# Decoder layer with 32 experts: the scatter products of an expert pair placed between the weight blocks of the next pair's gate/up product

## The chip, the cores and the metric

The kernel runs on one core of one Trainium2 chip. The metric is the device time of one execution in microseconds (us); lower is better. The times named as the median are of three executions; the profile is of a fourth one, whose time is given beside its span.

## The reference, cut to what matters

One layer of a decoder is computed for 256 prompt rows and 8 sample rows, T = 264 rows in all, of width 1024. After a convolution, two attentions and two normalisations each row goes to its 4 best of 32 experts. In the kernel the part around the change is the last one:

```python
def moe_ffn(x, w_router, b_router, w_gate_up, b_gate_up, w_down, b_down):
    ...
    logits = (xf @ w_router + b_router).astype(jnp.float32)
    top_logit, top_idx = lax.top_k(logits, TOP_K)
    gates = jax.nn.softmax(top_logit, axis=-1)
    ...
    def expert_block(args):
        xblk, e = args
        gu = xblk @ w_gate_up[e] + b_gate_up[e]
        g, u = jnp.split(gu, 2, axis=-1)
        g = jnp.minimum(g, SWIGLU_LIMIT)
        u = jnp.clip(u, -SWIGLU_LIMIT, SWIGLU_LIMIT)
        act = (u + 1.0) * g * jax.nn.sigmoid(SWIGLU_ALPHA * g)
        return act @ w_down[e] + b_down[e]
    ...
    y = jnp.zeros((T + 1, D_MODEL), yb.dtype).at[buf_tok].add(yb * buf_gate[:, None].astype(yb.dtype))
```

All is in float32. The gate/up weights of one expert are 1024 x 2048 numbers, 8 MB, and the down weights 1024 x 1024, 4 MB.

## The kernel before

Ahead of the experts the kernel computes the dense layers and the attentions; the change doesn't touch them. Then it works through the experts in 16 pairs. An expert has 64 slots for rows, so a pair fills the 128 partitions of one tile. For each pair, TensorE (PE) does this, in the function `pair(r, j)`, with `it = 2 * r + j`:

- gate/up of the first expert (`gate_up`, L1730): first a small bf16 product for the bias, then 8 blocks c = 0 to 7. A block is one loaded item of 1 MB of weights, and 4 matmuls with 512 columns each, two beside each other in the two halves of the array's columns. They add up in PSUM banks 0 and 1.
- the scatter (`scatter`, L1762): 8 products, c = 0 to 7. Each takes 128 of the 1024 output columns of the pair before (`yb`, copied from PSUM by ScalarE, ACT) and spreads them with the selection matrix `SelT` to the 264 rows of the layer. They use PSUM banks 2 and 3 in turn. VectorE (DVE) adds each one to the running sum `xT` (`add_scattered`, L1350), and product c waits until the addition of product c - 2 is done (semaphore `e_y_out`).
- 3 small transposes that make the next `SelT` (L1797), 4 transposes of the activations of the first expert (`turn_act`, L1739), which ACT copies to `actT` (L917), and then `down` (L1752): 4 items of 1 MB, 8 matmuls' worth of each half.
- gate/up of the second expert, then the gathering of the rows of the next pair (`gather`, L1702 and L1704), `turn_act`, and `down` of the second expert.

DVE works in the order in which its loop is written: for the first expert `clamp` (L1333 writes g2, L1335 writes u2) and `swiglu` (L1339, L1343), then `add_scattered`, then the copies of `SelT` (L1363 to L1365), the next selection matrices, then `clamp` and `swiglu` of the second expert. ACT computes the sigmoid between them (L911). `clamp` waits for `e_gu`, which the last matmul of gate/up raises; `turn_act` waits for `e_act`, which L1343 raises. So the order on DVE decides when PE gets the additions and when it gets the activations.

The weights come by DMA from the sync queue (SP). There are 16 items of room. `round_loads` walks over the items in order: before item m it waits in `item_read` until PE is through with the item that lay there (`e_wu` after each of the blocks 0 to 6, `e_gu` after block 7, `e_du` and `e_dn` for down). An expert has 12 items, all experts together 384, and the first 16 are loaded before the experts start. SP's order is fixed: while it waits for one item's room it issues nothing behind it.

In the last pair (`last=True`) the gathering is left out, and `sum_turned` (L1776) lays the running sum into the PSUM banks of the last normalisation.

Of the kernel before, what the change touches and what calls it, by code (L numbers as in the profile page):

```python
# [25 lines left out]
P = 128  # L26
D = 1024
DC = D // P
NP_ = 256
NS = 8  # L30
T = NP_ + NS
# [105 lines left out]
def decoder_layer(nc, x_prompt, x_sample, mem_prompt, cache_win_k, cache_win_v, state_conv, cache_mem_k,  # L137
# [4 lines left out]
    with ctx:  # L142
# [15 lines left out]
        ps = ctx.enter_context(nc.psum_tensor("ps", [P, 8, 512], F32))  # L158
# [115 lines left out]
        yb = view(m0 + 3584, 2, 512)  # L274
# [655 lines left out]
        def _(dve):  # L930
# [424 lines left out]
                dve.sem_inc(first, 1)  # L1355
            pairs = dve.value_load(nswi[0:1, 0:1], min_val=16, max_val=80)
            with dve.Fori(0, pairs) as it:
                clamp(2 * it)
                swiglu(2 * it)
                add_scattered(it)  # L1360

                dve.wait_ge(e_st, it + 1)
                nc.vector.tensor_copy(SelT[:, 0, :], ps[:, 3, 0:T]).then_inc(e_st_out, 1)  # L1363
                nc.vector.tensor_copy(SelT[0:64, 1, :], ps[64:P, 3, 0:T]).then_inc(e_st_out, 1)
                nc.vector.tensor_copy(SelT[64:P, 1, :], ps[0:64, 3, 0:T]).then_inc(e_st_out, 1)  # L1365

                q = ((it + 1) % 16) * 2
                dve.wait_ge(e_pos, it + 1)
                dve.wait_ge(e_selg, it + 1)
                select(q)  # L1370
                advance(q, it + 2)
                clamp(2 * it + 1)
                pick_biases(q)
                swiglu(2 * it + 1)
# [5 lines left out]
        def _(pe):  # L1380
# [334 lines left out]
            ins.then_inc(s_rt, 1)  # L1715
            pe.wait_ge(s_nsw, 4)

            def gate_up(r, k):


                a = k % 2
                for c in range(-1, 8):
                    if c >= 0:
                        item_arrived(pe, r, PER_EXPERT * k + c)
                        w, x = expert_slot(PER_EXPERT * k + c), xTe[:, c, SLOTS * a:SLOTS * a + SLOTS]
                    else:
                        w, x = bgu3[0:3 * NX, :], selE[0:3 * NX, a, :]
                    for gu in range(2):
                        for j in range(2):
                            ins = mm(ps[64 * j:64 * j + 64, gu, :], x,  # L1730
                                     w[:, D * gu + 512 * j:D * gu + 512 * j + 512], start=(c < 0), stop=(c == 7),
                                     skip_group_check=True)
                    if 0 <= c < 7:
                        ins.then_inc(e_wu, 1)
                ins.then_inc(e_gu, 1)

            def turn_act():
                for q in range(4):
# [14 lines left out]
                                     start=(m == 0), stop=(m == 7), skip_group_check=True)  # L1753
                    ins.then_inc(e_du if i < 3 else e_dn, 1)

            def scatter():

                for c in range(DC):
                    half = c // 4
                    if c >= 2:  # L1760
                        pe.wait_ge(e_y_out, scattered[0] + c)
                    mm(ps[:, 2 + c % 2, 0:T], yb[:, half, P * (c % 4):P * (c % 4) + P], SelT[:, half, :],  # L1762
                       start=True, stop=True).then_inc(e_y, 1)

            scattered = [0]
            pe.sem_inc(e_at, 1)
            pairs = pe.value_load(nswi[0:1, 0:1], min_val=16, max_val=80)
            last_round = pe.value_load(nswi[0:1, 2:3], min_val=7, max_val=39)
# [10 lines left out]
            def pair(r, j, last=False):  # L1779

                it = 2 * r + j
                scattered[0] = DC * it
                pe.wait_ge(e_gx_out, it + 1)
                pe.wait_ge(e_sb, it + 1)
                pe.wait_ge(e_u2, 2 * it + 1)
                gate_up(r, 2 * j)
                pe.wait_ge(s_first, 16)
                pe.wait_ge(s_rt_out, 6)
                pe.wait_ge(s_alpha, 1)
                pe.wait_ge(e_yb, it + 1)  # L1790
                pe.wait_ge(e_st_out, 3 * it + 1)
                pe.wait_ge(e_at_out, 2 * it + 1)
                scatter()
                pe.wait_ge(e_y_out, DC * it + (DC + 1))
                pe.wait_ge(e_selg, it + 1)
                for t, (t0, n) in enumerate(TCH):
                    ins = tp(ps[:, 3, t0:t0 + n], SelG[0:n, t].rearrange("p a s -> p (a s)"), ident[0:n, 0:n])  # L1797
                ins.then_inc(e_st, 1)
                pe.wait_ge(e_act, 2 * it + 2)
                turn_act()  # L1800
                pe.wait_ge(e_at_out, 2 * it + 2)
                down(r, 2 * j)
                if last:
                    sum_turned(0, 0)
                    sum_turned(0, 1)
                    pe.wait_ge(e_st_out, 3 * it + 4)
                    sum_turned(1, 1)
                pe.wait_ge(e_u2, 2 * it + 2)
                gate_up(r, 2 * j + 1)
                if last:  # L1810
                    pe.wait_ge(e_u2, 2 * it + 3)
                    sum_turned(2, 0)
                    sum_turned(2, 1)
                else:
                    pe.wait_ge(e_sel, it + 2)
                    gather()
                pe.wait_ge(e_act, 2 * it + 3)
                turn_act()
                pe.wait_ge(e_at_out, 2 * it + 3)
                if last:  # L1820
                    sum_turned(1, 0)
                down(r, 2 * j + 1)
# [44 lines left out]
```

## Time and profile before

| | us |
|---|---|
| median of 3 runs | 1408.44 |
| the three runs | 1408.44, 1399.79, 1411.55 |
| the profiled execution | 1414.02 |
| its span | 1412.1 |
| PE busy | 1224.5 (87% of the span) |
| DVE busy | 376.2 (27%) |
| ACT busy | 210.1 (15%) |
| mean granted clock of TensorE | 0.954 of full speed |
| moved from HBM | 479.40 MB |

The profiled execution took 1.9 us more than its span, and 5.6 us more than the median. Busy shares are means over stages that have different limits, so they say little by themselves: which wait ends last in a stage has to be read from the chain of waits and from the timeline of that stage. Line numbers are those of the kernel before. A float32 matmul leaves two records in the trace, so that a block of 4 matmuls is 8 records and a scatter product 2; their durations overlap, and some records are missing.

### The profile page before, as it was taken

How to read it: one execution, taken by the hardware profiler on the slowest of the kernel's cores; microseconds unless marked ns; L12 is line 12 of the kernel's file. 1: busy time of each engine (PE TensorE's matmuls, PEld its weight loads, DVE VectorE, ACT ScalarE, POOL GpSimd, SP SyncE). 2: the span in 40 equal slices, each digit the busy share in tenths (PEclk: the TensorE clock that was granted, in tenths of full speed). 3: DMA queues.
4: the chain of work that ended last, by engine and by line, in shares of the span. 5: the costliest groups of instructions: out<-in, count | busy, mean ns of one | idle time of the engine just before them, and what ended most of it. 6: DMA issues, size and time to landing. Idle time of an engine off the chain costs nothing.

```text
span 1412.1 us, 16873 instructions
## 1 busy us (share of the span) xinstructions
PE 1224.5 (87%) x6509; PEld 617.4 (44%) x6509; DVE 376.2 (27%) x843; ACT 210.1 (15%) x370; POOL 78.8 (6%) x61
## 2 busy tenths in 40 slices
PE   3896997995887999999899998999889898898986
PEld 2894443874674334333433343333433333333332
DVE  3365433117325221202212032021220202212023
ACT  3441222022312010010110101101001010100001
POOL 2014300004001000000000000000000000000001
PEclk7998999998997999999999999999999999999999
DMA  9885799515991999999999999999999999999993
GB/s 289 178 255 164 181 164 337 179 65 201 364 417 74 364 418 416 416 419 417 419 418 416 417 419 417 419 417 416 418 419 418 419 417 416 418 418 418 417 416 130
DMA packets 104709, 487.17 MB, mean 345 GB/s; under 512 B 8948, under 2 KB 10636, under 8 KB 71296
## 3 DMA queue, kind: packets, MB, share of 16 engines
q1 hardware_dynamic: 99296, 469.47, 85.3%
q0 software_dynamic: 3824, 15.62, 4.2%
q10 hardware_dynamic: 1552, 1.57, 0.4%
q8 instruction: 25, 0.41, 0.1%
q14 instruction: 12, 0.10, 0.0%
HBM read 479.40 MB, written 7.24 MB: 345 GB/s over the span
## 4 chain that ended last, share of the span: by engine, by line
PE 56%; SPq 24%; DVE 9%; issue 4%; ACT 3%; DMA 3%; POOL 1%; DVEq 0%; POOLq 0%
PE ps L1730 19%; SPq L569 13%; SPq L565 11%; PE ps L1433 11%; PE ps L1752 10%; PE ps L1464 4%; PE ps L1762 3%; PE ps L1702 2%; DMA ring<-in_w_gate_up_dram 2%; PE ps L1583 1%; DVE arena L1350 1%; DVE ring L1064 1%; ACT arena L917 1%; PE ps L1418 1%; DMA arena<-in_b_gate_up_dram 1%
## 5 line engine op out<-in xcount | busy, mean ns | idle before, releaser
L1730 PE MATMUL ps<-ring,arena 128*64 128x512 f32 x1536 | 340.1, 594 | 11.7 <-DMA ring<-in_w_gate_up_dram 11.7
L1333 DVE TENSOR_SCALAR arena<-ps 128x512 f32<-128x512 f32 x32 | 22.2, 693 | 703.0 <-PE ps L1730 703.0
L1730 PEld LDWEIGHTS ps<-ring,arena 128*64 128x64 f32 x1536 | 108.8, 137 | 228.1 <-issue 188.4
L1752 PE MATMUL ps<-ring,arena 128*64 128x512 f32 x768 | 170.1, 596 | 22.6 <-ACT arena L917 22.6
L1762 PE MATMUL ps<-arena 128*128 128x264 f32 x256 | 92.4, 507 | 34.5 <-DVE arena L1350 33.6
L1752 PEld LDWEIGHTS ps<-ring,arena 128*64 128x64 f32 x768 | 53.1, 137 | 124.2 <-issue 95.9
L911 ACT ACTIVATE arena<-arena 128x512 f32<-128x512 f32 x32 | 20.2, 632 | 578.3 <-DVE arena L1333 578.3
L1433 PE MATMUL ps<-arena,ring 128*128 128x264 f32 x384 | 89.2, 395 | 5.1 <-DVE arena L1120 3.7
L1464 PE MATMUL ps<-x_split,w_split 128*128 128x264 f32 x576 | 75.0, 294 | 21.1 <-DVE w_split L949 21.1
L1762 PEld LDWEIGHTS ps<-arena 128*128 128x128 f32 x256 | 52.2, 239 | 80.5 <-DVE arena L1350 62.6
L1730 PE MATMUL ps<-late,arena 128*64 128x512 f32 x384 | 85.3, 593 | 0.3 <-DMA late<-in_w_gate_up_dram 0.3
L1464 PEld LDWEIGHTS ps<-x_split,w_split 128*128 128x128 f32 x576 | 73.7, 197 | 22.1 <-issue 14.7
L1433 PEld LDWEIGHTS ps<-arena,ring 128*128 128x128 f32 x384 | 74.5, 195 | 19.2 <-DVE arena L1120 3.9
L1350 DVE TENSOR_TENSOR arena<-arena,ps 128x264 f32<-128x264 f32 x128 | 53.6, 429 | 36.3 <-PE ps L1762 35.2
L1702 PE MATMUL ps<-arena 128*128 128x128 bf16 x768 | 55.5, 225 | 8.2 <-DVE arena L1313 8.2
L1433 PE MATMUL ps<-ring,arena 128*128 128x512 f32 x128 | 60.4, 628 | 0.0
L1702 PEld LDWEIGHTS ps<-arena 128*128 128x128 bf16 x768 | 50.8, 101 | 20.4 <-issue 20.4
L730 POOL TENSOR_TENSOR late<-late,arena 128x1024 f32<-128x1024 f32 x1 | 2.0, 1994 | 960.5 <-ACT late L848 960.5
L1730 PEld LDWEIGHTS ps<-late,arena 128*64 128x64 f32 x384 | 27.5, 137 | 55.4 <-issue 53.6
L1730 PE MATMUL ps<-arena 96*64 96x512 bf16 (+1 forms) x256 | 48.2, 486 | 0.9 <-ACT arena L906 0.9
L669 POOL TENSOR_TENSOR ring<-ring 128x1536 f32<-128x1536 f32 (+1 forms) x11 | 42.3, 3858 | 47.3 <-DMA ring<-in_cache_win_k_dram 25.1
L949 DVE TENSOR_TENSOR w_split<-ring,w_split 128x1024 fp32r<-128x1024 f32 x24 | 35.4, 1484 | 35.2 <-ACT w_split L758 35.1
(264 smaller groups left out, 990.6 us busy)
## 6 DMA issues: line engine op xcount, KB each, us to landing
ring<-in_w_gate_up_dram SPq DMA_DIRECT2D x192, 1024.0 KB, 20.5
ring<-in_w_down_dram SPq DMA_DIRECT2D x96, 1024.0 KB, 24.4
late<-in_w_gate_up_dram SPq DMA_DIRECT2D x48, 1024.0 KB, 19.3
late<-in_w_down_dram SPq DMA_DIRECT2D x24, 1024.0 KB, 23.4
arena<-in_w_gate_up_dram SPq DMA_DIRECT2D x16, 1024.0 KB, 19.2
ring<-in_w_in_dram SPq DMA_DIRECT2D x12, 1024.0 KB, 22.2
ring<-in_cache_mem_k_dram SPq DMA_DIRECT2D x8, 1024.0 KB, 4.9
ring<-in_cache_mem_v_dram SPq DMA_DIRECT2D x8, 1024.0 KB, 8.1
```

The costliest lines, as they stand in the source:

```text
L565: sp.dma_start(dst, src).then_inc(done, 16)
L569: sp.dma_start(dst.rearrange("p (k n) -> p k n", k=2), src).then_inc(done, 16)
L669: nc.gpsimd.tensor_tensor(k, k, q.unsqueeze(1).broadcast_to((P, 2, width)), ALU.mult).then_inc(s_kq, 1)
L949: nc.vector.tensor_tensor(w_lo[p % 2], win_piece(p), w_hi[p % 2].bitcast(F32), ALU.subtract).then_inc(s_wlo, 1)
L1333: nc.vector.tensor_scalar(g2, ps[:, 0, :], 7.0, None, ALU.min).then_inc(e_g2, 1)
L1350: nc.vector.tensor_tensor(xT[:, c, :], xT[:, c, :], ps[:, 2 + c % 2, 0:T], ALU.add).then_inc(e_y_out, 1)
L1433: ins = mm(out(n), lhs(w, k, kk), rhs(w, k, kk), start=(kk == 0), stop=(kk == 7))
L1464: ins = mm(ps[:, n % 4, 0:T], w[p % 2][:, cols], x[kk], start=(kk == 0 and m == 0), stop=(kk == 7 and m == 2))
L1702: mm(out, x3[:, t, k, P * c:P * c + P], Sel[:, t].rearrange("p a s -> p (a s)"), start=(t == 0 and k == 0), stop=False)
L1730: ins = mm(ps[64 * j:64 * j + 64, gu, :], x, w[:, D * gu + 512 * j:D * gu + 512 * j + 512], start=(c < 0), stop=(c == 7), skip_group_check ...
L1752: ins = mm(ps[64 * j:64 * j + 64, 4 + half, :], x, w[:, kk, 512 * half:512 * half + 512], start=(m == 0), stop=(m == 7), skip_group_check= ...
L1762: mm(ps[:, 2 + c % 2, 0:T], yb[:, half, P * (c % 4):P * (c % 4) + P], SelT[:, half, :], start=True, stop=True).then_inc(e_y, 1)
```

## The change

The 8 scatter products leave their place behind the gate/up product of the first expert and go between its blocks: product c - 1 stands behind block c, for c = 1 to 7, and the product 7 behind product 6 at the end. `e_gu` is still raised by the last matmul of block 7, ahead of the products 6 and 7. The waits that stood ahead of the scatter (for `yb`, `SelT` and the first values) now stand ahead of product 0, behind block 1. On DVE `add_scattered(it)` moves ahead of `clamp(2 * it)`. The numbers of the instructions and what they compute stay the same; so do the orders of SP and ACT.

```diff
--- before.py
+++ after.py
@@ -1355,9 +1355,9 @@
                 dve.sem_inc(first, 1)
             pairs = dve.value_load(nswi[0:1, 0:1], min_val=16, max_val=80)
             with dve.Fori(0, pairs) as it:
+                add_scattered(it)
                 clamp(2 * it)
                 swiglu(2 * it)
-                add_scattered(it)
 
                 dve.wait_ge(e_st, it + 1)
                 nc.vector.tensor_copy(SelT[:, 0, :], ps[:, 3, 0:T]).then_inc(e_st_out, 1)
@@ -1715,7 +1715,7 @@
             ins.then_inc(s_rt, 1)
             pe.wait_ge(s_nsw, 4)
 
-            def gate_up(r, k):
+            def gate_up(r, k, scattered=None):
 
 
                 a = k % 2
@@ -1732,7 +1732,12 @@
                                      skip_group_check=True)
                     if 0 <= c < 7:
                         ins.then_inc(e_wu, 1)
-                ins.then_inc(e_gu, 1)
+                    if c == 7:
+                        ins.then_inc(e_gu, 1)
+                    if scattered is not None and c > 0:
+                        scatter(scattered, c - 1)
+                if scattered is not None:
+                    scatter(scattered, DC - 1)
 
             def turn_act():
                 for q in range(4):
@@ -1753,16 +1758,21 @@
                                      start=(m == 0), stop=(m == 7), skip_group_check=True)
                     ins.then_inc(e_du if i < 3 else e_dn, 1)
 
-            def scatter():
-
-                for c in range(DC):
-                    half = c // 4
-                    if c >= 2:
-                        pe.wait_ge(e_y_out, scattered[0] + c)
-                    mm(ps[:, 2 + c % 2, 0:T], yb[:, half, P * (c % 4):P * (c % 4) + P], SelT[:, half, :],
-                       start=True, stop=True).then_inc(e_y, 1)
-
-            scattered = [0]
+            def scatter(it, c):
+
+                half = c // 4
+                if c == 0:
+                    pe.wait_ge(s_first, 16)
+                    pe.wait_ge(s_rt_out, 6)
+                    pe.wait_ge(s_alpha, 1)
+                    pe.wait_ge(e_yb, it + 1)
+                    pe.wait_ge(e_st_out, 3 * it + 1)
+                    pe.wait_ge(e_at_out, 2 * it + 1)
+                if c >= 2:
+                    pe.wait_ge(e_y_out, DC * it + c)
+                mm(ps[:, 2 + c % 2, 0:T], yb[:, half, P * (c % 4):P * (c % 4) + P], SelT[:, half, :],
+                   start=True, stop=True).then_inc(e_y, 1)
+
             pe.sem_inc(e_at, 1)
             pairs = pe.value_load(nswi[0:1, 0:1], min_val=16, max_val=80)
             last_round = pe.value_load(nswi[0:1, 2:3], min_val=7, max_val=39)
@@ -1779,18 +1789,10 @@
             def pair(r, j, last=False):
 
                 it = 2 * r + j
-                scattered[0] = DC * it
                 pe.wait_ge(e_gx_out, it + 1)
                 pe.wait_ge(e_sb, it + 1)
                 pe.wait_ge(e_u2, 2 * it + 1)
-                gate_up(r, 2 * j)
-                pe.wait_ge(s_first, 16)
-                pe.wait_ge(s_rt_out, 6)
-                pe.wait_ge(s_alpha, 1)
-                pe.wait_ge(e_yb, it + 1)
-                pe.wait_ge(e_st_out, 3 * it + 1)
-                pe.wait_ge(e_at_out, 2 * it + 1)
-                scatter()
+                gate_up(r, 2 * j, scattered=it)
                 pe.wait_ge(e_y_out, DC * it + (DC + 1))
                 pe.wait_ge(e_selg, it + 1)
                 for t, (t0, n) in enumerate(TCH):
```

PE, the first pair as it stands ahead of the loop's repetition, before: the blocks of gate/up (L1730), then the scatter (L1762; L1761 and L497 are the reckoning of the values waited for).

```order
238 L1730 MATMUL ps<-ring,arena 64x512 x8
239 L497 REGISTER_ALU
240 L1730 MATMUL ps<-ring,arena 64x512 x4
241 L1791 ISA
242 L1762 MATMUL ps<-arena 128x264 x2
243 L1761 ISA
244 L1762 MATMUL ps<-arena 128x264
245 L1761 REGISTER_ALU
246 L1762 MATMUL ps<-arena 128x264
247 L1761 REGISTER_ALU
248 L1762 MATMUL ps<-arena 128x264
```

All 8 products stand together behind the last block. PE, the same place of the changed kernel, where the scatter's line is L1773 and its waits are L1769 and L1772:

```order
234 L1730 MATMUL ps<-late,arena 64x512 x4
235 L1769 ISA
236 L1773 MATMUL ps<-arena 128x264
237 L1730 MATMUL ps<-late,arena 64x512 x4
238 L1773 MATMUL ps<-arena 128x264
239 L1730 MATMUL ps<-late,arena 64x512 x4
240 L1772 ISA
241 L1773 MATMUL ps<-arena 128x264
...
254 L1730 MATMUL ps<-ring,arena 64x512 x4
255 L1772 REGISTER_ALU
256 L1773 MATMUL ps<-arena 128x264
258 L1773 MATMUL ps<-arena 128x264
```

Six of the products have moved ahead of the last block, and two follow it. DVE, the start of its loop over the pairs, before: the clamps and the activation (L1333 to L1343), then the additions (L1350).

```order
344 L1333 TENSOR_SCALAR arena<-ps 128x512
345 L1335 TENSOR_SCALAR arena<-ps 128x512
346 L1338 REGISTER_ALU
347 L1339 SCALAR_TENSOR_TENSOR arena<-arena 128x512
348 L1343 TENSOR_TENSOR arena<-arena 128x512
349 L1347 ISA
350 L1350 TENSOR_TENSOR arena<-arena,ps 128x264
351 L1349 REGISTER_ALU
352 L1350 TENSOR_TENSOR arena<-arena,ps 128x264
```

DVE, the end of the additions and what follows them in the changed kernel:

```order
356 L1350 TENSOR_TENSOR arena<-arena,ps 128x264
357 L1349 REGISTER_ALU
358 L1350 TENSOR_TENSOR arena<-arena,ps 128x264
359 L1332 ISA
360 L1333 TENSOR_SCALAR arena<-ps 128x512
361 L1335 TENSOR_SCALAR arena<-ps 128x512
362 L1338 REGISTER_ALU
363 L1339 SCALAR_TENSOR_TENSOR arena<-arena 128x512
364 L1343 TENSOR_TENSOR arena<-arena 128x512
365 L1362 REGISTER_ALU
```

The eight additions now stand ahead of the clamps of the same pair.

## Rows read from the trace of the kernel before

**Rows 1.** The page, GB/s in 40 equal slices of the span

```profile
GB/s 289 178 255 164 181 164 337 179 65 201 364 417 74 364 418 416 416 419 417 419 418 416 417 419 417 419 417 416 418 419 418 419 417 416 418 418 418 417 416 130
```

**Rows 2.** Busy time by stretch; last columns granted clock, DMA share, GB/s

```profile
600.00:700.00 100.00, 92.23 (x506) 37.52 (x503) 17.19 (x34) 10.71 (x13) 0.00 (x0) 0.98 1.02 418
960.00:1300.00 340.00, 303.20 (x1612) 122.03 (x1612) 66.91 (x138) 33.90 (x42) 0.00 (x0) 0.98 1.02 418
1385.00:1390.00 5.00, 4.32 (x33) 2.91 (x32) 0.99 (x2) 0.59 (x1) 0.00 (x0) 1.00 0.13 50
```

**Rows 3.** The chain of waits: start us, us, what

```profile
849.18 7.09 PE ps L1752 x32
...
877.87 0.73 PE ps L1762 x2
...
907.17 7.09 PE ps L1752 x32
...
1052.88 5.53 SPq L569
...
1113.13 5.54 SPq L569
```

**Rows 4.** Timeline of one pair: start us, us, engine, line, operation, idle before

```profile
869.41 0.14 PEld L1730 LDWEIGHTS ps<-ring,arena 128*64 128x64 f32 x2 [0.28 <-issue]
870.37 1.16 PE L1762 MATMUL ps<-arena 128*128 128x264 f32 x4
870.49 0.69 DVE L1333 TENSOR_SCALAR arena<-ps 128x512 f32<-128x512 f32 x1 [23.38 <-PE ps L1730]
...
872.54 0.69 DVE L1343 TENSOR_TENSOR arena<-arena 128x512 f32<-128x512 f32 x1
...
879.63 0.66 PE L1739 MATMUL ps<-arena 128*128 128x128 f32 x4
...
881.03 1.94 PE L1752 MATMUL ps<-arena 128*64 128x512 f32 x8 [0.75 <-ACT arena L917]
```

**Rows 5.** Timeline of the last pair

```profile
1343.93 1.94 PE L1730 MATMUL ps<-ring,arena 128*64 128x512 f32 x8 [0.55 <-DMA ring<-in_w_gate_up_dram]
...
1346.41 1.94 PE L1730 MATMUL ps<-ring,arena 128*64 128x512 f32 x8 [0.55 <-DMA ring<-in_w_gate_up_dram]
...
1348.28 1.16 PE L1762 MATMUL ps<-arena 128*128 128x264 f32 x4
...
1358.98 1.94 PE L1752 MATMUL ps<-arena 128*64 128x512 f32 x8 [0.75 <-ACT arena L917]
...
1388.89 7.09 PE L1752 MATMUL ps<-ring,arena 128*64 128x512 f32 x32
```

**Rows 6.** Timeline of the first pair, and one stretch of it by busy time

```profile
466.23 1.16 PE L1762 MATMUL ps<-arena 128*128 128x264 f32 x4
...
476.69 7.09 PE L1752 MATMUL ps<-ring,arena 128*64 128x512 f32 x32 [0.68 <-ACT arena L917]
...
478.67 5.48 SPq L565 DMA_DIRECT2D ring<-in_w_gate_up_dram  x4
...
477.00:478.00 1.00, 1.00 (x6) 0.29 (x4) 0.85 (x2) 0.00 (x0) 0.00 (x0) 1.00 0.00 0
```

**Rows 7.** The page's groups: busy us, mean ns of one, idle before

```profile
L1762 PEld LDWEIGHTS ps<-arena 128*128 128x128 f32 x256 | 52.2, 239 | 80.5 <-DVE arena L1350 62.6
...
L1350 DVE TENSOR_TENSOR arena<-arena,ps 128x264 f32<-128x264 f32 x128 | 53.6, 429 | 36.3 <-PE ps L1762 35.2
```

**Rows 8.** Granted clock by stretch, columns as in Rows 2

```profile
873.50:874.00 0.50, 0.37 (x1) 0.32 (x2) 0.41 (x2) 0.00 (x0) 0.00 (x0) 0.86 1.03 426
...
877.00:877.50 0.50, 0.50 (x3) 0.40 (x2) 0.12 (x1) 0.00 (x0) 0.00 (x0) 0.73 1.19 492
```

**Rows 9.** Timeline behind a second expert's down product

```profile
971.95 0.60 PE L1730 MATMUL ps<-arena 96*64 96x512 bf16 x4
972.17 1.01 ACT L922 COPY arena<-ps 128x1024 f32<-128x1024 f32 x1 [7.19 <-PE ps L1752]
```

## The prediction

> **What bounds the kernel now.** I read the page first, then busy time by stretch, then the chain of waits, and last the timelines of a first, a middle and the last expert pair. By its busy share (87%, in the table) PE looks like the bound, but the page's GB/s slices stay at 416 to 419 from the fifteenth slice to the last but one [rows 1]. The stretches say the same: 418 GB/s and a full DMA share both where PE is busy 92.23 of 100 us and where it is busy 303.20 of 340 [rows 2]. The chain shows two regimes. Up to about 960 us it runs through PE, with a pair period of 907.17 - 849.18 = 58.0 us; from there it runs through the sync queue, with a period of 1113.13 - 1052.88 = 60.25 us [rows 3]. A pair has 24 items of 1 MB (1.0486 million bytes): 24 x 1.0486 / 60.25 = 0.418 MB per us, which is the rate of the stretches. So the loads run without a hole, at one item in 2.5 us, from the first pair to about 1386 us, where the DMA share drops to 0.13 [rows 2]. In the first half PE only eats a stock of loaded items faster than it is refilled, and in the second half it waits for weights. Time that PE saves in the middle pairs buys nothing. Only two places count: the **last pair**, where PE works behind the last load it waited for, and the **first pair**, where PE decides when the loads can start again.
>
> **What is around the scatter.** In the pair at 870 us the first two scatter products start at 870.37, at once behind the last block. The third one needs an addition, and DVE makes additions only behind the clamps and the activation. From 870.37 to the start of down at 881.03 it is 10.66 us [rows 4]. In the last pair it is 1358.98 - 1348.28 = 10.70, in the first pair 476.69 - 466.23 = 10.46 [rows 5, 6].
>
> **The new way from the last block to down.** Behind the last block only the products 6 and 7 are left. Two products take 1.16 us to their end [rows 4]. The additions of the products 0 to 5 run beside the blocks, and that of product 7 follows its product with 0.43 us, the mean of an addition [rows 7]. Now DVE may clamp: from the start of L1333 to the end of L1343 it is 872.54 + 0.69 - 870.49 = 2.74 us; then come the turning of the activations and ACT's copy of them, 881.03 - 879.63 = 1.40 us to down [rows 4]. The sum is 1.16 + 0.43 + 2.74 + 1.40 = 5.73, with some hundredths for each hand-over between engines 5.8 us. The three small transposes for `SelT` fit into PE's idle time before the turning. So the additions ahead of the clamp cost the activation 1.5 us, and yet the way is 4.9 us shorter, 4.65 in the first pair.
>
> **The clock takes a part back.** PE is idle between the last scatter or transpose and the turning. Today the same idle, some 2.1 us between the second and third product, is followed by the lower level of the granted clock: from the two half-microsecond rows, 0.86 at 873.5 and 0.73 at 877.0, it stood at 0.50, which is 1.2 GHz, from 873.86 to 877.27, so 3.4 us [rows 8]. The same half-microsecond reading finds this in 13 of the 16 pairs, the first at 471 and the last at 1351.7. In the changed kernel PE is idle from 1.6 + 0.6 = 2.3 us after the last block (transposes done) to 4.4 us, again 2.1 us. I take it that the clock falls there too. 3.4 us at half clock cost at most 1.7 us; the copy by ACT lies in them and costs nothing more. I take 1.4, with 0 and 1.7 as the ends.
>
> **Cost of a product between two blocks.** One product more in a row costs 1.16 - 0.73 = 0.43 us of PE [rows 3, 4]. The change from a block to a product cost 0.10: the weight loads of a block come every 0.43 us, the last at 869.41, and the product starts at 870.37, 0.96 later instead of 0.86 [rows 4]. No row shows a product followed by a block of gate/up; the ends are 0 and another 0.1 to 0.5, and I take 0, since PE's stream goes on without a gap elsewhere. So one insertion is 0.53 us, six are 3.2.
>
> **Last pair.** There PE is paced by the loads: its blocks start at 1343.93 and 1346.41, 2.48 apart, and the next work follows a block's start by 1348.28 - 1346.41 = 1.87 [rows 5]. The free 0.61 us hold a product of 0.43 with 0.18 to spare. So the last block is as late as before, at the same time of the loads, the insertions are free, and the gain is 10.70 - 5.8 - 1.4 = **3.5 us** (3.2 to 4.9). Is something else late next? The 16 items behind that block arrive every 2.48 us, the last at 1346.41 + 39.7 = 1386.1; down of the last expert, which starts at 1388.89 and wants its last item 5.3 us later [rows 5], would start at 1385.4 and want it at 1390.7. For the last expert's gate/up, whose last item arrives at 1346.41 + 12 x 2.48 = 1376.2, there is a margin of a good microsecond. The loads stop the gain only beyond some 5 us.
>
> **First pair.** All 16 items are in when the experts start. The 8 blocks free 8 items; once these are moved the DMA engines stand still (0 GB/s from 477 to 478) until PE has finished the first item of down and SP issues again at 478.67 [rows 6]. Every microsecond by which down starts earlier moves the whole stream of 368 loads. But here PE is not paced by loads, so the insertions count: 4.65 - 3.2 = 1.45 us. With the fallen clock the turning and the first item of down take up to 1.3 us more: **0.15 us** are left (0 to 1.45). The blocks free an item every 1.77 + 0.53 = 2.3 us (down, of the same 1 MB items, takes 7.09 us for four [rows 3]), still under the 2.5 us of a load.
>
> **The 14 pairs between**: nothing. They would save PE 0.2 to 1.5 us each, and PE then waits that much longer for its next item, or eats its stock sooner.
>
> **The waits that moved.** Ahead of product 0 stands the wait for `yb`, with blocks 2 to 7 queued behind it on PE, and SP waits for those blocks. ACT has copied `yb` 1.2 us after gate/up starts (972.17 + 1.01 against 971.95) [rows 9], and product 0 comes two blocks, 4 us, after that start: covered. Without cover each microsecond would cost one in the first pair. `SelT` and `b_down` are older still. DVE stands in the additions while the blocks run; behind them are only the clamps, which need the last block anyway.
>
> **The sum** is 3.5 + 0.15, so about 3.7 us: the profiled execution would go from 1414.02 to 1410.3. That execution is 5.6 above the median of 1408.44; I take the gain off the median: **1404.8 us**.
>
> **The rivals.**
> *The clock stays up* behind the shorter, broken idle, as it did in 3 of 16 pairs. Then the last pair gives 4.9 and the first 1.45, together 6.3 us: 1402.1. Against it: the idle is as long as today.
>
> *The weights' loads show (the slower side).* Each product sits between blocks that use the array in another way. If PE could not load the weights of a product, and those of the next block, behind running matmuls, an insertion would cost two loads of 0.24 [rows 7] and one of 0.14 [rows 4] more, 0.62 us. In the first pair the blocks would end 6 x 0.62 = 3.7 us later and the loads would start again 0.15 - 3.7 = 3.6 us later than today; in the last pair (0.62 - 0.18) x 6 = 2.6 us of the 3.5 would go. The sum is -3.6 + 0.9: 2.7 us slower, 1411.1. It decides from 0.39 us per insertion on, where 3.65 = 6 x 0.39 + 6 x 0.21. Against it speaks the 0.10 us of the change from block to product [rows 4], where the first load was hidden. The Trainium skill, "TensorE: Matmul & The Clock Gate", Part 3, states that a weight load overlaps running matmuls only when it goes to another row group; all operands here use all 128 rows, so by that rule this rival would hold. The rows speak against the rule here.
>
> *PE sets the pace after all.* If the rate of 418 GB/s followed PE's demand, all 16 pairs would count: 16 x 1.45 = 23 us with the clock up, 1385; with the clock down 16 x 0.15 is lost among the rest. Against it: the same rate in both regimes [rows 2]. The Trainium skill, "Perfetto Trace Analysis", section "Optimization Strategies", advises to work on whatever the idle matmul engine waits for; read as a forecast, that advice is this rival, and the equal rates of this trace speak against it.
>
> **How the numbers follow.** Forecast (3 to 4 us) 0.6, clock up 0.2, weight loads shown 0.1, PE's pace 0.03; 0.07 for the rest. The first three span 1402.1 to 1411.1. The runs of one kernel lie between 1399.79 and 1411.55, so a median of a few can be off by some 4 us to either side; the slow case and a late run together are rare, and I give 1397 to 1412. About 1% (14 us) is what a measurement of this kernel can tell from no change: all cases but the pace of PE are within it. Faster by over 1%: 0.05; within 1%: 0.92; slower by over 1%: 0.03.
>
> **What would show it.** In the profile after: in the last pair down starts 5.8 to 7.5 us behind the last block; six products lie in the waits for loads, and the blocks there stay 2.48 us apart; the GB/s slices stay at 418, the chain goes over to the sync queue earlier than 960 us, and the second half's period stays at 60.25. In the first pair the hole without loads ends at about the same time. The clock falls once per pair, now at the turning. The forecast is wrong if the loads run faster than 418 GB/s, if blocks are further apart than 2.48 in the last pair, or if the end of the loads moves by more than 2 us.

## The result, and the profile after

The changed kernel takes 1435.03 us (median of 4 runs, 1430.61 to 1438.22) against 1406.33 for the kernel before (4 runs, 1399.79 to 1411.55). The ratio is 1.0208, with a 95% interval of 1.0166 to 1.025: it is slower by 2%, where no measurable change was forecast (1404.8 us, with a range of 1397 to 1412). The profiled execution took 1430.61 us, its span is 1428.7. All times and ratios here and below are of executions in the fast state; one of the ten of experiment 4 (2865.66 us, mean granted clock 0.449) was in the slow state and is not in its ratio.

The page of the changed kernel: busy time, GB/s in 40 slices, the costliest groups of gate/up and down, and the median time from issue to landing of a gate/up item.

```profile
PE 1254.8 (88%) x6509; PEld 600.9 (42%) x6509; DVE 374.4 (26%) x843; ACT 210.0 (15%) x370; POOL 78.6 (6%) x61
...
GB/s 289 177 256 153 183 194 360 119 89 221 408 350 162 361 416 411 418 418 418 416 417 418 418 418 416 417 418 419 418 417 417 418 419 418 418 416 417 417 273 31
...
L1730 PE MATMUL ps<-ring,arena 128*64 128x512 f32 x1536 | 351.3, 597 | 0.0
L1757 PE MATMUL ps<-ring,arena 128*64 128x512 f32 x768 | 187.1, 644 | 22.6 <-ACT arena L917 22.6
...
ring<-in_w_gate_up_dram SPq DMA_DIRECT2D x192, 1024.0 KB, 11.6
```

The rate of the loads is the same as in [rows 1], and yet the last two slices fall to 273 and 31: the last weights land at 1382.8 us, 46 us before the kernel ends. In the kernel before they landed at 1386.9, 25 us before its end. Gate/up (L1730) has no idle time before its matmuls now; in the kernel before this group waited 11.7 us for loads. An item lands 11.6 us after its issue, against 20.5 before. So in the changed kernel the loads do not set the end. The stretches say the same (columns as in [rows 2]); the second one shows PE at work with nearly all weights loaded:

```profile
960.00:1300.00 340.00, 316.55 (x1635) 119.25 (x1633) 60.21 (x124) 32.69 (x40) 0.00 (x0) 0.96 1.02 418
...
1380.00:1390.00 10.00, 10.00 (x62) 5.06 (x60) 0.00 (x0) 0.00 (x0) 0.00 (x0) 1.00 0.08 33
```

The chain of waits of the second pair, start and us. It never goes over to the sync queue, in contrast to [rows 3]; down is now L1757, the scatter L1773.

```profile
505.17 3.87 PE ps L1730 x20
509.04 0.64 PE ps L1773 x2
509.68 1.87 PE ps L1730 x8
511.55 0.64 PE ps L1773 x2
512.19 1.87 PE ps L1730 x8
...
524.10 1.10 PE ps L1773 x4
...
529.94 9.85 PE ps L1757 x32
539.79 14.17 PE ps L1730 x68
...
558.84 7.09 PE ps L1757 x32
565.93 3.87 PE ps L1730 x20
```

From here to the last pair the period is (1347.95 - 505.17) / 14 = 60.2 us; it was 58.0 [rows 3]. A block and a product now take 1.87 + 0.64 = 2.51 us together, where a block in an unbroken row takes 1.72 (in the timeline four of them take 6.87 us). The first down takes 9.85 us here and 7.09 for the second expert.

The way from the last block to down, in the timeline of the same pair, which answers to [rows 4]:

```profile
524.03 1.16 PE L1773 MATMUL ps<-arena 128*128 128x264 f32 x4
524.78 0.88 DVE L1350 TENSOR_TENSOR arena<-arena,ps 128x264 f32<-128x264 f32 x2 [2.08 <-PE ps L1773]
525.57 0.69 DVE L1333 TENSOR_SCALAR arena<-ps 128x512 f32<-128x512 f32 x1
...
527.62 0.69 DVE L1343 TENSOR_TENSOR arena<-arena 128x512 f32<-128x512 f32 x1
...
528.37 0.82 PE L1744 MATMUL ps<-arena 128*128 128x128 f32 x4 [2.06 <-DVE arena L1343]
...
529.94 3.68 PE L1757 MATMUL ps<-arena 128*64 128x512 f32 x8 [0.75 <-ACT arena L917]
```

It is 529.94 - 524.03 = 5.9 us, close to the 5.8 worked out; over the 16 pairs it is 5.7 to 6.2. PE is idle 2.06 us before the turning (L1744), as worked out too. What follows it is larger than I took it. The granted clock of this pair by stretch (third column from the right):

```profile
528.50:529.00 0.50, 0.50 (x4) 0.29 (x4) 0.47 (x2) 0.00 (x0) 0.00 (x0) 0.72 1.00 401
529.00:535.00 6.00, 5.25 (x13) 1.50 (x14) 1.75 (x5) 0.59 (x1) 0.00 (x0) 0.50 1.02 406
...
535.50:536.00 0.50, 0.50 (x4) 0.14 (x2) 0.00 (x0) 0.00 (x0) 0.00 (x0) 0.95 1.22 492
```

The lower level (0.50, that is 1.2 GHz) holds from 528.72 to 535.55, 6.8 us, twice as long as in [rows 8]. Read in the same way over all 16 pairs, it comes in every one, 10 times for 6.8 us and 6 times for 3.4: 88.8 us in all, against 44.4 in the kernel before. Most of it now lies in down.

### The profile page after: what moved, and what is told of

The parts are those of the page before. It is cut to its first block, busy times and chain, and to the rows that moved or that the text cites. A ratio compares the mean times of both kernels' runs of the same rounds, so it can differ in the third digit from the quotient of the medians.

```text
span 1428.7 us, 16873 instructions
## 1 busy us (share of the span) xinstructions
PE 1254.8 (88%) x6509; PEld 600.9 (42%) x6509; DVE 374.4 (26%) x843; ACT 210.0 (15%) x370; POOL 78.6 (6%) x61
## 4 chain that ended last, share of the span: by engine, by line
PE 81%; DVE 9%; ACT 4%; issue 3%; DMA 2%; POOL 1%; SPq 0%; DVEq 0%; POOLq 0%
PE ps L1730 33%; PE ps L1757 18%; PE ps L1433 10%; PE ps L1773 6%; PE ps L1464 4%; PE ps L1702 3%; ACT arena L917 1%; DMA ring<-in_cache_mem_v_dram 1%; PE ps L1744 1%; PE ps L1583 1%; DVE ring L1064 1%; DVE arena L1343 1%; DVE arena L1339 1%; DVE arena L1333 1%; DVE arena L1335 1%
## 5 line engine op out<-in xcount | busy, mean ns | idle before, releaser
L1730 PE MATMUL ps<-ring,arena 128*64 128x512 f32 x1536 | 351.3, 597 | 0.0
L1757 PE MATMUL ps<-ring,arena 128*64 128x512 f32 x768 | 187.1, 644 | 22.6 <-ACT arena L917 22.6
L1730 PEld LDWEIGHTS ps<-ring,arena 128*64 128x64 f32 x1536 | 102.4, 136 | 192.4 <-issue 188.1
L1350 DVE TENSOR_TENSOR arena<-arena,ps 128x264 f32<-128x264 f32 x128 | 55.2, 431 | 410.4 <-PE ps L1773 410.2
L1333 DVE TENSOR_SCALAR arena<-ps 128x512 f32<-128x512 f32 x32 | 22.1, 689 | 362.9 <-PE ps L1730 362.9
L1757 PEld LDWEIGHTS ps<-ring,arena 128*64 128x64 f32 x768 | 56.8, 148 | 137.7 <-issue 109.1
L1730 PE MATMUL ps<-late,arena 128*64 128x512 f32 x384 | 88.6, 596 | 0.0
L1773 PE MATMUL ps<-arena 128*128 128x264 f32 x256 | 86.9, 431 | 0.0
L1464 PEld LDWEIGHTS ps<-x_split,w_split 128*128 128x128 f32 x576 | 73.5, 196 | 22.1 <-issue 14.7
L1773 PEld LDWEIGHTS ps<-arena 128*128 128x128 f32 x256 | 39.4, 188 | 91.9 <-issue 90.9
L1744 PE MATMUL ps<-arena 128*128 128x128 f32 x128 | 22.7, 305 | 33.0 <-DVE arena L1343 33.0
L1730 PE MATMUL ps<-arena 96*64 96x512 bf16 (+1 forms) x256 | 48.2, 486 | 0.9 <-ACT arena L906 0.9
L1757 PE MATMUL ps<-late,arena 128*64 128x512 f32 x192 | 48.1, 655 | 0.0
L1730 PEld LDWEIGHTS ps<-late,arena 128*64 128x64 f32 x384 | 25.9, 136 | 51.5 <-issue 51.5
## 6 DMA issues: line engine op xcount, KB each, us to landing
ring<-in_w_gate_up_dram SPq DMA_DIRECT2D x192, 1024.0 KB, 11.6
```

The source lines that it names most:

```text
L1333: nc.vector.tensor_scalar(g2, ps[:, 0, :], 7.0, None, ALU.min).then_inc(e_g2, 1)
L1350: nc.vector.tensor_tensor(xT[:, c, :], xT[:, c, :], ps[:, 2 + c % 2, 0:T], ALU.add).then_inc(e_y_out, 1)
L1464: ins = mm(ps[:, n % 4, 0:T], w[p % 2][:, cols], x[kk], start=(kk == 0 and m == 0), stop=(kk == 7 and m == 2))
L1730: ins = mm(ps[64 * j:64 * j + 64, gu, :], x, w[:, D * gu + 512 * j:D * gu + 512 * j + 512], start=(c < 0), stop=(c == 7), skip_group_check ...
L1744: ins = tp(ps[:, 2, P * q:P * q + P], act_[:, P * q:P * q + P], ident)
L1757: ins = mm(ps[64 * j:64 * j + 64, 4 + half, :], x, w[:, kk, 512 * half:512 * half + 512], start=(m == 0), stop=(m == 7), skip_group_check= ...
```

## The experiments

The **stage** below is the time from the first gate/up product of the first pair to the start of the last down product, read in each profile's timeline. It leaves out the work ahead of the experts, which no experiment touches and after which the first gate/up product starts at 438.2 to 451.9 us, and the last normalisation, the same in all. It is 1388.89 - 451.94 = 936.95 us before and 1405.48 - 445.53 = 959.95 after. Each stage is read from one profile; two profiles of the same kernel (experiments 3 and 9) are 0.3 us apart. PE's **period** is the mean time from one pair to the next, over the pairs in which PE waits for no load.

**1. The idle time before the turning filled.** Theory A, formed from the profile: PE's own period became longer than the loads allow. Theory B: the loads come later.

```diff
                 ins.then_inc(e_st, 1)
+                stay_awake(8, ps[:, 6, 0:P])
                 pe.wait_ge(e_act, 2 * it + 2)
                 turn_act()
```

> The changed kernel, with 8 idle float32 matmuls of the identity (0.21 us each at full clock) behind the three transposes for SelT, in PE's idle time of 2.06 us before the first expert's turning. Theory A: the slowdown comes from PE's own pair period, which went from 58.1 to 60.2 us, of which the low clock in down takes 2.2 (down 9.3 us instead of 7.09), while the loads allow some 58.7 a pair. With the idle filled the clock stays up, down takes 7.09 again, the period of the first half falls to about 57.9 and the time to that of the kernel before or a few us below it (ratio 0.995 to 1.000). Theory B: the loads are the cause, because blocks free their items later; then the clock changes little and the ratio stays near 1.02. Theory C: fillers don't hold the clock; down stays at 9 us and the ratio at 1.02.

Measured: ratio 0.9984 (0.9957 to 1.001). Its timeline, with the fillers (L1418), the turning and down:

```profile
642.53 2.05 PE L1418 MATMUL ps<-arena 128*128 128x128 f32 x16
...
644.67 0.66 PE L1744 MATMUL ps<-arena 128*128 128x128 f32 x4
...
646.08 1.94 PE L1757 MATMUL ps<-arena 128*64 128x512 f32 x8 [0.75 <-ACT arena L917]
...
652.99 0.61 PE L1730 MATMUL ps<-arena 96*64 96x512 bf16 x4
```

Down takes 6.9 us to the next gate/up, the clock stays at 1.00 in all pairs, the period is 57.8 and the stage 933.3 us. More work on PE makes the changed kernel 2% faster: theory C is out, and A fits.

**2. Two products at a time**, three insertions instead of six.

```diff
-                    if scattered is not None and c > 0:
+                    if scattered is not None and c > 0 and c % 2 == 0:
+                        scatter(scattered, c - 2)
                         scatter(scattered, c - 1)
                 if scattered is not None:
+                    scatter(scattered, DC - 2)
                     scatter(scattered, DC - 1)
```

> The changed kernel, with the products two by two: 0 and 1 behind block 2, 2 and 3 behind block 4, 4 and 5 behind block 6, 6 and 7 behind block 7 as now. Three insertions instead of six. Theory A with a price of 0.31 us for each change of the array's use (0.10 from block to product, 0.21 back): gate/up gets 0.93 us shorter, the period 60.2 falls to 59.3, and the time to some +9 us against the kernel before (ratio 1.005 to 1.010). If the price hangs on each product and not on each change, gate/up stays at 18.9 us and the ratio at 1.02.

Measured: 0.9995 (0.9971 to 1.002), less than expected. The price does hang on the change of use:

```profile
511.29 1.16 PE L1775 MATMUL ps<-arena 128*128 128x264 f32 x4
512.38 3.65 PE L1730 MATMUL ps<-ring,arena 128*64 128x512 f32 x16
515.96 1.16 PE L1775 MATMUL ps<-arena 128*128 128x264 f32 x4
```

Two products take 1.09 us to the next block, 2 x 0.43 + 0.23; two blocks take 3.58 to the next product, 2 x 1.72 + 0.14. So one interruption costs 0.37 us besides the products' columns, for one product or for two. Gate/up and the way to down shrink by 1.1 us. The clock's part shrinks too, which I hadn't counted: down takes 0.4 us less on average than in the changed kernel, and the period is 58.6 on average. The stage is 936.9, equal to that of the kernel before: its chain runs through PE up to 1289 us and through the sync queue behind it, so this kernel lies at the edge between the two bounds.

**3. Both**, the diffs of 1 and 2 together.

> Both: products two by two, and the fillers before the turning. Theory A: PE's period would be 60.2 - 2.2 - 0.9 = 57.0, well below what the loads allow, so the loads set the pace from earlier on, and the time is that of the kernel with fillers alone or 1 us below: 0.994 to 0.999 of the kernel before. Theory B: near 1.02.

Measured: 0.999 (0.9965 to 1.0016). PE's period is 56.7 us until about 850, then the loads' 60.25 holds. Stage 931.4.

**4. The order of DVE alone.** All 8 products behind block 7, the additions ahead of the clamps.

```diff
-                    if scattered is not None and c > 0:
-                        scatter(scattered, c - 1)
                 if scattered is not None:
-                    scatter(scattered, DC - 1)
+                    for c in range(DC):
+                        scatter(scattered, c)
```

> One part alone: all 8 products stand behind block 7 as in the kernel before, but DVE adds before it clamps. No product between blocks, so no price for the changes of use. From the last block to down it should be 0.75 + 7 x 0.62 + 0.43 for the additions, 2.74 for the activation and 1.40 to down, 9.7 us. Theory A: PE's idle before the turning is 2 us as in the changed kernel, so the clock falls there and down takes 9.3; period 58.1 - 10.7 + 9.7 + 2.2 = 59.3, +9 us (ratio 1.005 to 1.010). If the clock stays up: period 57.1 and no slowdown.

Measured: 1.0043 (1.002 to 1.0066), a slowdown as expected, a little smaller.

```profile
515.62 4.93 PE L1772 MATMUL ps<-arena 128*128 128x264 f32 x16
...
523.73 0.65 PE L1743 MATMUL ps<-arena 128*128 128x128 f32 x4 [2.06 <-DVE arena L1343]
...
525.14 2.47 PE L1756 MATMUL ps<-arena 128*64 128x512 f32 x6 [0.75 <-ACT arena L917]
```

The way is 9.5 us, a good microsecond shorter than before; the idle of 2.06 us stands at the same place as in the changed kernel, and down takes 8.3 to 9.9 us behind it. The period is 58.9 us, the stage 938.3, and no load is waited for. So the DVE order by itself, without any product between blocks, moves the low clock into down and gives back more than it gains.

**5 and 6. Less to load**, in the changed kernel (5) and in the kernel before (6).

```diff
-                    src = down_rows[bass.ds(e, 1), (i - 8) * 2 * P:(i - 7) * 2 * P, :].rearrange(
-                        "a (k p) n -> p (a k) n", p=P)
-                    sp.dma_start(dst.rearrange("p (k n) -> p k n", k=2), src).then_inc(done, 16)
+                    ...
+                    src = down_rows[bass.ds(e, 1), (i - 8) * 2 * P:(i - 8) * 2 * P + P, :].rearrange(
+                        "a p n -> (a p) n")
+                    sp.dma_start(dst[:, 0:D], src).then_inc(done, 16)
```

> The changed kernel with less to load: of every down item beyond the 16 loaded ahead only the first of its two 128-row parts is loaded, 20 MB a pair instead of 24; the products run on what lies in the rest. So the results of the experts are not the reference's. Theory A (PE's period of 60.2 us sets the end): nothing changes against the changed kernel, ratio 1.015 to 1.025 to the kernel before. Theory B (loads come too late because of the later releases): the time falls by 15 us or more.

> The kernel before with the same reduced loads. Here the loads set the pace from 960 us on at 60.25 us a pair; without them PE's 58.1 holds to the end, 5 to 6 pairs x 2.2 us less, so 10 to 12 us faster (ratio 0.991 to 0.994). Theory A then has the changed kernel 16 x 2.1 = 33 us behind its like. If the time doesn't fall, the loads were not the bound of the kernel before either.

The diff is cut: the branch left out loads the items of the first 16 as before. The added lines shift the numbers behind them by 5, so that down is L1757 in 6 and L1762 in 5.

Measured: 1.0195 (1.0143 to 1.0247) for 5, so the changed kernel gains nothing from a sixth less to load; 0.9919 (0.9884 to 0.9954) for 6. The rate of the loads in 5 and the chain in 6 in the second half, where [rows 3] have the sync queue:

```profile
GB/s 291 177 270 162 174 233 354 76 139 241 409 282 175 307 316 394 327 400 316 306 380 332 402 312 335 360 326 408 313 359 342 324 399 318 383 322 316 394 148 31
```

```profile
1223.35 7.09 PE ps L1757 x32
...
1281.28 7.09 PE ps L1757 x32
```

In 6 PE keeps its period of 57.8 us to the end; stages 960.7 and 922.3. These two decide between A and B: the kernel before was bound by its loads, the changed one is bound by PE, 38 us apart where loads don't matter.

**7 and 8. Work added to the kernel before**, nothing moved: 3 and 10 idle matmuls at the start of each pair.

```diff
                 pe.wait_ge(e_gx_out, it + 1)
+                stay_awake(3, ps[:, 6, 0:P])
```

> The kernel before with 3 idle float32 matmuls of the identity (0.64 us) on PE at the start of each pair. Theory A: the period goes from 58.1 to 58.7, which the loads just allow; the time stays within 3 us of the kernel before (ratio 0.998 to 1.003).

> The kernel before with 10 idle float32 matmuls (2.13 us) on PE at the start of each pair, nothing moved. Theory A: the period becomes 60.2, as in the changed kernel, and the time rises like there, by 20 to 25 us (ratio 1.015 to 1.018). If PE's time in the middle pairs bought and cost nothing, as the prediction had it, the ratio stays within 1.003.

Measured: 1.0014 (0.9984 to 1.0044) and 1.0158 (1.011 to 1.0205). The chain of 8, the fillers of two pairs (the second kernel of the pair has `stay_awake(10, ...)`):

```profile
614.37 2.43 PE ps L1418 x20
...
674.67 2.43 PE ps L1418 x20
```

60.3 us apart here, 59.7 on average, since some pairs keep the clock. The stage is 1388.14 - 438.15 = 950.0, and the last slices of the page read 351 and 31 GB/s, as in the changed kernel. With 3 fillers a pair whose clock stays up takes 57.6 us instead of 56.7, but the clock falls in 8 pairs instead of 13 (27.3 us at the lower level in all instead of 44.4), so that the period is only 58.1, and the stage 937.3. So 1.9 us more of PE in each pair are enough for a slowdown of the observed kind, and 0.3 us more cost nothing.

**9. The better version again**, the kernel of 3 in more rounds.

> The same kernel as the one with products two by two and fillers, with more rounds. In its first profile the time from the first gate/up to the last down was 931.4 us against 936.95 in the kernel before, PE's period 56.7 against 57.8. If only the last and the first pair pay, the gain is these 5 us: ratio 0.994 to 0.998. If the work ahead of the experts hides it, as in the first measurement (0.999), the interval holds 1.

Measured: 0.9964 (0.9938 to 0.9991), 1400.02 us against 1405.57; taken with the 0.999 of experiment 3, the gain is about a quarter of a per cent. The chain is in the hands of the loads, 60.26 us apart, and the stage 931.8.

```profile
1046.66 6.37 SPq L569
...
1106.92 6.34 SPq L569
```

**10. The kernel before with its own idle filled.**

```diff
                 for c in range(DC):
                     half = c // 4
+                    if c == 2:
+                        stay_awake(8, ps[:, 6, 0:P])
                     if c >= 2:
```

> The kernel before, with 8 idle matmuls of the identity (1.7 us) only in PE's idle time of 2.1 us between the second and the third product; nothing else is changed. The low clock of the scatter goes, the way from the last block to down takes 9.35 us instead of 10.66, PE's period in the first half 56.7 instead of 57.8. If saved time of PE in the middle buys nothing, the loads take over some pairs earlier and only the last pair's 1.3 us are gained: ratio 0.998 to 1.000. If it counted in each pair it would be 13 x 1.3 = 17 us, 0.988.

Measured: 0.9991 (0.9964 to 1.0018). The scatter behind the fillers, and down:

```profile
630.32 3.63 PE L1764 MATMUL ps<-arena 128*128 128x264 f32 x12 [0.32 <-DVE arena L1350]
...
636.40 1.94 PE L1752 MATMUL ps<-arena 128*64 128x512 f32 x8 [0.75 <-ACT arena L917]
```

PE's period falls to 56.6 us in the first seven pairs, and then the loads hold it at 60.2. Stage 934.3: of the 17 us that PE saves only 2.6 arrive. They come from the two places that the prediction counted. In the first pair, whose first gate/up product starts at 442.94, SP issues again 25.5 us after it, where it was 26.7 before:

```profile
468.47 0.34 SPq L565 DMA_DIRECT2D ring<-in_w_gate_up_dram  x1
```

In the last pair the way from the last block to down is 9.35 us instead of 10.70. That is 1.2 + 1.35 = 2.55 us.

All stages beside PE's own mean period:

| kernel | PE's mean period | stage | ratio |
|---|---|---|---|
| before, less to load (6) | 57.8 | 922.3 | 0.9919 |
| two and filled (3, 9) | 56.7 | 931.4, 931.8 | 0.999, 0.9964 |
| changed, filled (1) | 57.8 | 933.3 | 0.9984 |
| before, filled (10) | 56.6 | 934.3 | 0.9991 |
| before | 57.8 | 936.95 | 1 |
| before + 3 (7) | 58.1 | 937.3 | 1.0014 |
| two at a time (2) | 58.6 | 936.9 | 0.9995 |
| DVE order alone (4) | 58.9 | 938.3 | 1.0043 |
| before + 10 (8) | 59.7 | 950.0 | 1.0158 |
| changed | 60.2 | 959.95 | 1.0208 |
| changed, less to load (5) | 60.2 | 960.7 | 1.0195 |

Where the loads set the pace from some pair on, the period is the mean of the pairs ahead of that one. Where PE sets the pace to the end (4, 5, 6, 8 and the changed kernel), the stage is 15 periods and the last pair, from its first gate/up product to the last down 54.7 to 57.7 us long. Where the loads set it, the stage lies at 931 to 937 us whatever PE's period is. With the last pair of the changed kernel (57.7 us) the two meet at a period of (936.95 - 57.7) / 15 = 58.6 us.

## Why the prediction was wrong

**The step that failed is "The 14 pairs between: nothing".** It was right for saved time: experiment 10 saved PE 1.2 us in each pair, and no gain can be told from the noise in the ratio. It was taken to hold whatever the period became, and there it has an edge that the trace of the kernel before already gave. Its last pair starts here:

```profile
1330.44 0.60 PE L1730 MATMUL ps<-arena 96*64 96x512 bf16 x4
```

From there to the last down it is 1388.89 - 1330.44 = 58.45 us, waits for loads included. With a period of 58.0 [rows 3] PE alone would need at most 15 x 58.0 + 58.45 = 928.5 us for a stage that took 937. The margin of the loads over PE was at least 8.5 us, 0.6 a pair. Experiment 6 measured PE alone at 922.3 us, a margin of 14.7 us or 0.9 for each of the 16 pairs. PE of the changed kernel needs 960.0 us, 37.7 more than that; the loads had covered 14.7 of these, and 23.0 are left, the growth of the stage. I never worked out that margin; I called time of PE worthless because the loads were busy all the time, and their being busy only says that there was still something to fetch. With the period of 57.7 us that the prediction's own terms give, the statement would have stood; two of these terms carried it over the edge.

**The period itself** was forecast (by the prediction's own terms, 58.0 - 4.9 + 3.2 + 1.4) at 57.7, and is 60.2. (The same terms give a middle pair a saving of 0.3 us, or 1.7 with the clock up; the 0.2 to 1.5 of the prediction are the first pair's.) Two terms were too small:

- *Cost of a product between two blocks.* I took 0.53 us each. It is 2.51 - 1.72 = 0.79: 0.43 for the columns, 0.15 from block to product instead of 0.10, and 0.21 from product back to block, where I took 0 (its range went to 0.5). Six times 0.26 is 1.6 us a pair. Experiment 2 shows that it hangs on the interruption, and that half as many interruptions are enough to end the slowdown.
- *The clock takes a part back.* I took 1.4 us and called 1.7 the most. Down takes 9.3 us on average instead of 7.09, 2.2 us, since the low level lasts 6.8 us in 10 of 16 pairs. The bound of 1.7 rested on the length of 3.4 us that all 13 cases of the kernel before had. Experiment 1 shows this term alone to be enough: without it the change is no longer slower.

From the last block to down the forecast held (5.8 forecast, 5.7 to 6.2 measured). The two losses less the gain are, against the kernel before, 6 x 0.79 - (10.66 - 5.9) + 2.2 = 2.2 us, which is 60.2 - 58.0.

**Last pair.** The forecast gain of 3.5 us rested on PE waiting for its loads there. The chain of the changed kernel has blocks 2.51 us apart, where 2.48 were forecast, with no wait for a load, and down 10.09 us long:

```profile
1360.00 1.87 PE ps L1730 x8
1362.51 1.87 PE ps L1730 x8
...
1372.56 10.09 PE ps L1757 x32
```

With the pace of the loads back (experiments 1, 3 and 9) the stage is 3.7, 5.5 and 5.2 us shorter than before. These kernels keep the clock up, and for that case the prediction had 6.3 us: 4.9 in the last pair and 1.45 in the first. In 1, which has the six insertions, the last pair's way from the last block to down is 5.75 us instead of 10.70, so the 4.9 are there. But its gate/up takes 19.0 us up to the product behind the last block instead of 17.85 (1348.28 - 1330.44), for the last pair of the kernel before waits only 3.6 us for loads in that stretch, and six insertions of 0.79 us take 4.7. The first pair gives nothing: SP issues again 26.7 us after the first gate/up product, as before. So 4.95 - 1.2, about 3.7 us, are left. The mechanism of the last pair was right, the insertions were not free, and in the changed kernel it all came to nothing because another bound had taken over.

**First pair.** Forecast was a gain of 0.15 us in the time until the loads go on.

```profile
464.58 1.16 PE L1773 MATMUL ps<-arena 128*128 128x264 f32 x4
...
470.25 8.78 PE L1757 MATMUL ps<-ring,arena 128*64 128x512 f32 x32 [0.68 <-ACT arena L917]
...
473.56 13.14 SPq L565 DMA_DIRECT2D ring<-in_w_gate_up_dram  x8
```

SP issues again 473.56 - 445.53 = 28.0 us after the first gate/up product, against 478.67 - 451.94 = 26.7 [rows 6]: 1.3 us later, where 0.15 earlier was forecast; the difference is about the six times 0.26. It costs nothing here, where the last weights land 46 us before the end.

**The rivals.** The one on the slower side had the right mechanism in kind, a price of the interruption that had been taken for hidden, though its size was 0.26 over my price and not 0.62. I priced it at the first and the last pair only, 2.7 us, and said that it decides from 0.39 us on. Carried through all pairs it decides much earlier. That whole loads of weights stand bare the timeline doesn't show: in the changed kernel the load of a product and the product start together, and so do the load of a block and the block (the idle time noted is the weight path's own, behind the load before).

```profile
508.97 0.30 PEld L1773 LDWEIGHTS ps<-arena 128*128 128x128 f32 x2 [0.81 <-issue]
...
509.61 0.20 PEld L1730 LDWEIGHTS ps<-ring,arena 128*64 128x64 f32 x4 [0.35 <-issue]
```

The 0.64 us from one to the other are the product's 0.43 and 0.21 more, about the 0.19 us of one of its loads. That is as much as the trace says: which part of the change of use takes the time stays open. The rule of the Trainium skill, "TensorE: Matmul & The Clock Gate", Part 3 (a load overlaps running matmuls only in another row group), as I had priced it, would have put 0.62 us on my price for each interruption. The runs show 0.26 more for a single product, and for two products, with twice as many loads of 128 columns, the interruption of experiment 2 costs the same 0.37 us as for one. So in this trace most of the loads do overlap running matmuls, although these loads all use the same 128 rows; the row 1380:1390 above has PE busy for 10.00 of 10.00 us with 5.06 us of loads in them. "The clock stays up" did not hold in any pair. "PE sets the pace after all" came true in another sense than meant: not because the rate of the loads followed PE, it stayed at 418 GB/s, but because PE no longer emptied the stock of 16 items and so never waited for a load.

**What stays open.** The medians are 28.7 us apart, the stages 23.0. The lower end of the ratio's interval (1.0166) is 23.3 us, so the stages lie just below it, and with four executions of each kernel the 28.7 are probably somewhat high. Experiment 5, whose stage is that of the changed kernel within 0.7 us, is 23.0 us above the kernel before measured with it (14 executions). Whether the rest is the spread of the work ahead of the experts, one profile of each can't tell. It also stays open why the low clock lasts 3.4 us in some pairs and 6.8 in others.

## What to carry to other kernels

Where a stream of loads runs without a hole, saved time of the engine that eats them is worth nothing in the middle of the stream, but lost time isn't free: work out how much longer its period may get before it no longer catches up with the stock, from the whole stage and not from one pair (here 0.6 us of 58 by the trace, 0.9 when measured with less to load). When a stall is moved, look at what runs behind it: an idle of 2 us in front of short products that wait for DVE anyway cost 1.3 us of clock, the same idle in front of a dense stream of matmuls cost 2.2, and eight idle matmuls in it gave all of it back. Products put between blocks that use the array in another way were cheaper in groups: 0.37 us for each interruption, for one product or two.

## What the runs showed of the hardware

A break of TensorE's work of 2.06 us, with one of 0.5 before it and one of 0.7 behind it, was followed by the lower level of the clock in 16 of 16 pairs of the changed kernel, for 3.4 us or for 6.8. I had not expected the second length: with the level down, the stream of down's matmuls, busy throughout, ran at 1.2 GHz for up to 6.1 us before it rose. Filled with 8 float32 matmuls of 128 columns, the same place kept 2.4 GHz in every pair (experiments 1, 3 and 9). An interruption of a stream of matmuls with 64-column weights, two beside each other, by products with 128-column weights costs 0.37 us: 0.15 going in and 0.21 to 0.23 coming back, for one product or two.
